# Second layer's modulation parts 2 to 5 by TensorE beside the convolution, fewer expert slots in the first sweep

## The chip, the core and the metric

The kernel runs on one NeuronCore of one Trainium2 chip. The metric is the device time of one execution in microseconds, as the median of several runs. All inputs are in the chip's memory (HBM) at the start, and the outputs are there at the end. The matrix products run on TensorE (PE), the element-wise work on VectorE (DVE), ScalarE (ACT) and GpSimd (POOL), and most transfers are issued by SyncE (SP).

## The reference

It is one step of a two-layer trunk on 384 tokens (128 context, 256 latent) of width 1024. What matters here:

```python
def adaln(cvec, w, b):
    m = jax.nn.silu(cvec) @ w + b                 # w: 1024 x 6144, two vectors cvec (c_ctx and c)
    return jnp.split(m[:, None, :], 6, axis=-1)
for l in range(DEPTH):                            # DEPTH = 2
    mp = adaln(c_ctx[None, :], mod_w[l], mod_b[l])
    ms = adaln(c, mod_w[l], mod_b[l])
    hp = modulate(rms_norm(xp, norm_mix_g[l]), mp[0], mp[1])
    ...                                           # layer 0: attention and pooling; layer 1: conformer_conv
    xp = xp + mp[2] * op
    hp = modulate(rms_norm(xp, norm_ffn_g[l]), mp[3], mp[4])
    xp = xp + mp[5] * peer(hp, ...)               # the same for the latent tokens with ms
def conformer_conv(h, w1, b1, w_dw, b_dw, ln_g, ln_b, w2, b2):
    a = h @ w1 + b1
    a = a[..., :CONV_DIM] * jax.nn.sigmoid(a[..., CONV_DIM:])
    a = depthwise_conv(a, w_dw, width=31) + b_dw
    a = jax.nn.silu(layer_norm(a, ln_g, ln_b))
    return a @ w2 + b2
```

`peer` picks 128 experts per token (8 heads, 16 each) out of 16384. It needs the dot product of the token with each expert's row of `peer_u`, and then the weighted sum of the rows of `peer_v`.

## The kernel before

The layout is transposed: `x[p, k, t]` holds channel 128 k + p of token t, so a row of 1024 channels is KC = 8 chunks of 128 partitions. Each engine has its own program, written out by hand. The order on an engine is the order of its code, and engines wait for one another by counting semaphores.

**Projections.** A block is a 128 x 1024 piece of a weight matrix (512 KB). SP loads it into one of four slots of `raw`, ACT rounds it into `w_hi`, POOL forms the rest `w_lo = raw - w_hi` (helper `low`), and PE multiplies: `project` issues 24 matmuls (8 chunks, 3 terms). The segments are in, out, wq0, u0, v0, w1 (16 blocks), w2 (8 blocks), wq1, u1, v1. In the u and v segments there are 128 blocks each.

**Experts of a layer.** For the 256 latent tokens the u and v tables are swept densely. In the u segment blocks 0 to 31 run while DVE finds the top keys (`top_keys`), blocks 32 to 95 run beside the building of the gate table (`with_table`), and blocks 96 to 127 are the tail (TAIL = 32). The v segment is the sweep: for each block DVE forms the weights `wf` from `a_in` and `g_in` (both read back from HBM), and PE runs `block_of`, 8 fp32 matmuls. For the 128 context tokens the experts' rows are fetched one slot at a time: POOL's `gather` is an indirect DMA of 128 rows of 8 KB (1 MB), into one of UVBUFS = 4 buffers, and it waits on `rows_used` until the row four slots earlier has been used. DVE's `step` makes the slot's dot product, ACT's `weight` bends and scales it, and DVE's `add_row` adds the row in the next step. Of the 128 slots of a layer 32 belong to the table blocks (one every two blocks), TAIL_STEPS to the tail and PER_EIGHT per eight blocks to the sweep.

**Modulation.** A block of `mod_w` is 512 KB: 128 output channels by 1024 inputs. DVE's `mod_group` takes the dot product of a block with one of the two conditioning vectors, held on all partitions in `c_all` (in `keys`), so a block takes two instructions; after four blocks `mod_bias` adds the bias. Part 0 of layer 0 (`shift_w`) is done by PE (`first_shift`). Of the other 88 blocks 32 are done in attention's stage (`mod_w`, slots in `hots`) and 56 in the first sweep (`mod_late`). DVE does 20 of the early blocks in `mod_four`, the last 12 in `late_mod`.

**Convolution (layer 1).** `blocks("w1")` projects 16 blocks in pairs. After each pair DVE's `product(k)` writes the gated chunk k into `a_pad`, and then issues 12 of its pending taps. The depthwise convolution of the 8 chunks is split: POOL does chunk 0 (31 taps of two instructions), DVE the chunks up to CONV_DVE, PE the rest, with 31 matmuls against diagonals that ACT makes. Then come the column sums for the layer norm (L1703 for the mean, L1707 for the squares), `blocks("w2")`, the next norm's column sums and `scores`.

```python
                for k in range(KC):
                    product(k)
                    if k >= CONV_POOL:
                        taps(12)
                taps(len(pending))
```

## Time and profile before

| what | value |
|---|---|
| median of 3 runs | 2520.72 us (2520.61 to 2526.32) |
| the profiled execution | 2531.83 us, span 2530.0 us |
| PE busy | 2294.8 us (91%) |
| DVE busy | 1735.4 us (69%) |
| POOL busy | 1180.4 us (47%) |
| ACT busy | 911.2 us (36%) |
| moved by DMA | 771.19 MB, 305 GB/s over the span |
| chain of waits | PE 55%, DMA 17%, DVE 13%, POOL 6% |

The shares are averages over stages with different limits, so each stage is read by itself, with the windows view (busy time of every engine in a stretch, the clock granted to TensorE, the share of time in which the 16 DMA engines were busy, and the rate). Matmul records overlap: the time from one start to the next is the pace, and the duration is the latency.

### The profile page before, as it was taken

What the parts mean: (1) busy time and instruction counts of PE and PEld (TensorE: products, weight loads), DVE (VectorE), ACT (ScalarE), POOL (GpSimd) and SP (SyncE); (2) the same over time, 40 slices, a digit from 0 to 9 for tenths busy, and PEclk for the clock granted to TensorE, in tenths of its full rate; (3) what the DMA queues carried; (4) which work ended last, traced back from release to release, by engine and by line L of the source; (5) the groups of instructions that cost most, each with busy time, mean ns of one, the idle gap of its engine ahead of it and who ended that gap; (6) DMA issues with size and microseconds to landing.
All of it is one profiled execution on the core that took longest, in us unless ns stands there. A gap on an engine that the chain in (4) does not pass through costs nothing.

```text
span 2530.0 us, 38376 instructions
## 1 busy us (share of the span) xinstructions
PE 2294.8 (91%) x11829; PEld 1693.0 (67%) x11829; DVE 1735.4 (69%) x3913; ACT 911.2 (36%) x1694; POOL 1180.4 (47%) x673
## 2 busy tenths in 40 slices
PE   6687999999998888888989889999999989999998
PEld 3676999999983333333459479989999944444443
DVE  7986798888435766677757856898885345545555
ACT  3253445666541111111033354656666410000002
POOL 2623487777782222222219635677777831111110
PEclk8898999999998999999999999999999999999999
DMA  7423368999999999999953023579999999999995
GB/s 300 158 77 125 109 225 286 381 390 375 379 412 398 400 396 402 386 394 401 394 187 122 9 67 117 183 254 369 383 386 376 391 366 400 400 398 408 400 399 188
DMA packets 195783, 771.19 MB, mean 305 GB/s; under 512 B 21728, under 2 KB 22880, under 8 KB 160224
## 3 DMA queue, kind: packets, MB, share of 16 engines
q1 hardware_dynamic: 120512, 402.81, 42.8%
q0 software_dynamic: 36864, 268.45, 26.8%
q10 hardware_dynamic: 38304, 98.71, 10.0%
q8 instruction: 45, 0.74, 0.1%
q14 instruction: 58, 0.48, 0.1%
HBM read 701.08 MB, written 68.81 MB: 304 GB/s over the span
## 4 chain that ended last, share of the span: by engine, by line
PE 55%; DMA 17%; DVE 13%; POOL 6%; issue 6%; ACT 2%; SPq 0%; ACTq 0%; DVEq 0%; POOLq 0%
PE ps L1785 26%; DMA raw<-in_v 12%; PE ps L1548 7%; PE ps L1549 7%; PE ps L1550 7%; POOL w_lo L602 5%; PE ps L1767 4%; DMA raw<-in_u 4%; DVE ps L1284 2%; DVE ps L1365 1%; DVE work L1367 1%; DVE ga L1084 1%; PE ps L1720 1%; ACT w_hi L728 1%; POOL work L674 1%
## 5 line engine op out<-in xcount | busy, mean ns | idle before, releaser
L602 POOL TENSOR_TENSOR w_lo<-raw,w_hi 128x1024 fp32r<-128x1024 f32 x330 | 802.9, 2440 | 514.1 <-ACT w_hi L728 511.6
L1785 PE MATMUL ps<-raw,work 128*128 128x512 f32 x2048 | 917.0, 608 | 92.5 <-DMA raw<-in_v 81.9
L1785 PEld LDWEIGHTS ps<-raw,work 128*128 128x128 f32 x2048 | 394.7, 195 | 613.5 <-issue 578.4
L1548 PE MATMUL ps<-h_hi,w_hi 128*128 128x256 f32 (+1 forms) x2560 | 773.9, 302 | 30.1 <-POOL w_lo L602 29.5
L1549 PE MATMUL ps<-h_lo,w_hi 128*128 128x256 f32 (+1 forms) x2560 | 754.0, 295 | 0.0
L1550 PE MATMUL ps<-h_hi,w_lo 128*128 128x256 f32 (+1 forms) x2560 | 753.8, 294 | 0.0
L1548 PEld LDWEIGHTS ps<-h_hi,w_hi 128*128 128x128 f32 x2560 | 491.9, 192 | 42.6 <-POOL w_lo L602 38.7
L1549 PEld LDWEIGHTS ps<-h_lo,w_hi 128*128 128x128 f32 x2560 | 492.5, 192 | 0.0
L1550 PEld LDWEIGHTS ps<-h_hi,w_lo 128*128 128x128 f32 x2560 | 491.4, 192 | 0.0
L728 ACT ACTIVATE w_hi<-raw 128x1024 fp32r<-128x1024 f32 x330 | 347.7, 1056 | 125.0 <-DMA raw<-in_u 49.0
L973 ACT ACTIVATE wgt<-dots (+1 forms) x256 | 53.2, 208 | 764.0 <-DVE uv_stat L1426 223.3
L620 POOL DMA_INDIRECT work<-in_uv,picked x64 | 73.7, 1151 | 245.4 <-DVE ps L1418 236.4
L620 POOL DMA_INDIRECT hots<-in_uv,picked x64 | 73.9, 1155 | 243.9 <-DVE ps L1418 232.8
L1445 DVE TENSOR_SCALAR hots<-ps,work 128x128 f32<-128x128 f32 x512 | 173.7, 401 | 0.0
L1469 DVE TENSOR_TENSOR work<-work,w_hi 128x256 f32<-128x256 f32 x128 | 53.7, 423 | 170.4 <-PE ps L1785 119.7
L993 ACT ACTIVATE work<-ps 128x512 f32<-128x512 f32 x128 | 145.8, 1139 | 66.9 <-PE ps L1767 65.0
L1469 DVE TENSOR_TENSOR work<-work 128x256 f32<-128x256 f32 x128 | 53.5, 423 | 166.9 <-PE ps L1785 125.5
L956 ACT ACTIVATE ga<-ps 128x256 f32<-128x256 f32 x256 | 97.7, 382 | 180.0 <-PE ps L1550 169.8
L1084 DVE CUSTOM_DVE_ANT_0 ga<-work,keys 128x1024 bf16<-128x1024 f32 x112 | 136.3, 1217 | 19.0 <-DMA work<-in_mod_w 11.7
L620 POOL DMA_INDIRECT hf<-in_uv,picked x64 | 71.9, 1124 | 152.6 <-DVE ps L1418 148.7
L1441 DVE TENSOR_TENSOR hots<-ps,work 128x512 f32<-128x512 f32 x128 | 87.9, 687 | 79.8 <-PE ps L1767 79.8
L620 POOL DMA_INDIRECT uv_stat<-in_uv,picked x64 | 71.5, 1117 | 141.5 <-DVE ps L1418 137.9
(199 smaller groups left out, 2524.7 us busy)
## 6 DMA issues: line engine op xcount, KB each, us to landing
raw<-in_u SPq DMA_DIRECT2D x256, 512.0 KB
raw<-in_v SPq DMA_DIRECT2D x256, 512.0 KB
a_dram<-ga ACTq DMA_DIRECT2D x128, 256.0 KB
g_dram<-work ACTq DMA_DIRECT2D x16, 2048.0 KB
work<-a_dram ACTq DMA_DIRECT2D x120, 256.0 KB
work<-in_mod_w SPq DMA_DIRECT2D x56, 512.0 KB, 14.5
hots<-in_mod_w SPq DMA_DIRECT2D x32, 512.0 KB, 3.6
raw<-in_wq SPq DMA_DIRECT2D x32, 512.0 KB
```

The costliest lines, as they stand in the source:

```text
L602: nc.gpsimd.tensor_tensor(w_lo[:, m % RING, :], raw[:, m % RING, :], w_hi[:, m % RING, :].bitcast(F32), ALU.subtract).then_inc(lo_ready, 1)
L620: nc.gpsimd.indirect_dma_start(out=uv_rows[q % UVBUFS], out_offset=None, in_=io[f"uv{layer}"], in_offset=bass.IndirectOffsetOnAxis(ap=pick ...
L728: nc.scalar.activation(w_hi[:, m % RING, :], raw[:, m % RING, :], ACT.Copy).then_inc(hi_ready, 1)
L993: nc.scalar.activation(stage[:, s, :, tok:tok + TOK].rearrange("p k t -> p t k"), ps[:, ACC, :].rearrange("p (t k) -> p t k", k=N_KEYS), A ...
L1084: nc.vector.tensor_tensor_reduce(unread[:, g, :], ring[:, k, :], c_all[:, g, :], 1.0, 0.0, ALU.mult, ALU.add, accum_out=sums[:, k, g:g + 1 ...
L1445: last = ts(oh1[:, b, q, :], iota_p, col_key[:, 0, tok], col_g[:, tok], ALU.is_equal, ALU.mult)
L1469: tt(wf[:, j % WBUFS, :].rearrange("p (c t) -> p c t", t=CHUNK), a_in[:, j % (2 * A_PAIRS), :].rearrange("p (c t) -> p c t", t=CHUNK), g_i ...
L1548: mm(out, w_hi[:, s, cols], h_hi[:, k, first:], start=n == 0, stop=False)
L1549: mm(out, w_hi[:, s, cols], h_lo[:, k, first:], start=False, stop=False)
L1550: last = mm(out, w_lo[:, s, cols], h_hi[:, k, first:], start=False, stop=n == KC - 1)
L1767: last = mm(ps[:, ACC, q * P:(q + 1) * P], oh2[:, b, q, :], oh1[:, b, q, :], start=True, stop=True)
L1785: last = mm(ps[:, Y_DENSE[NT - ND_TILES + t] + half, :], wf[:, b, t * P:(t + 1) * P], raw[:, s, half * 512:(half + 1) * 512], start=first, ...
```

## The change

Six things change together.

1. Parts 2 to 5 of layer 1's modulation (32 blocks) are no longer summed by DVE in the first sweep. A new array `part_w` holds them with inputs on the partitions, and PE's new `part_chunks` multiplies each chunk (128 inputs x 1024 outputs, 8 matmuls of 128 x 128 fp32 weights against two columns, `cvec`). Four chunks stand before w1, eight singly behind w1's blocks 5 to 12, eight before the mean, four before w2 and eight before layer 1's wq. SP loads them into five slots in `work`.
2. DVE's new `part_taken` adds the bias from PSUM. PE waits for the last one (`parts_taken`) before the wq1 projection.
3. Layer 0's sweep keeps 24 blocks of modulation instead of 56, two groups per four v blocks.
4. CONV_DVE is 7 instead of 6: DVE convolves six chunks, PE one, POOL one.
5. In layer 0 the sweep has 4 expert slots per eight blocks instead of 5, and the tail 32 instead of 16. Layer 1 stays.
6. `mod_four` reads the first vector from PSUM (`c_ps`), where ACT writes a second copy of it.

```diff
-CONV_DVE = 6
+CONV_DVE = 7
...
-SLOT_AT = (0, 2, 4, 5, 7)
-PER_EIGHT = len(SLOT_AT)
...
+SLOT_AT = ((0, 2, 4, 6), (0, 2, 4, 5, 7))
+PER_EIGHT = tuple(len(a) for a in SLOT_AT)
+TAIL_STEPS = tuple(SLOTS - TABLE_STEPS - N_KEYS // 8 * per for per in PER_EIGHT)
...
+SUM_PARTS = (1, 2, 3, 4, 5, 6, 7)
+PE_PARTS = (8, 9, 10, 11)
+PSLOTS = 5
+CHUNKS_NORM, CHUNKS_W1, CHUNKS_MEAN, CHUNKS_W2, CHUNKS_WQ = (range(a, b) for a, b in ((0, 4), (4, 12), (12, 20), (20, 24), (24, 32)))
+SUM_BLOCKS = len(SUM_PARTS) * KC
...
+            def part_chunks(chunks):
+
+                for n in chunks:
+                    since(sp, part_done, n - PSLOTS + 1)
+                    sp.dma_start(part_w[:, n % PSLOTS, :], one(io["part_w"], n)).then_inc(part_loaded[n % PSLOTS], 16)
...
+                    sp.wait_ge(rows_used, SLOTS)
+                    part_chunks(range(0, 5))
+                    stream("w1", RING, 1, 1)
+                    for n in range(5, 16):
+                        part_chunks([n])
+                        stream("w1", n, 1, 1)
...
+            nc.scalar.activation(c_ps, c_all[:, 0, :], ACT.Silu).then_inc(c_ready, 1)
...
-                        mod_group(i, MSLOTS, 0, k, g)
+                        mod_group(i, MSLOTS, 0, k, g, first=c_ps)
...
+            def part_taken(part, bank, col):
+
+                dve.wait_ge(part_done, (part - PE_PARTS[0] + 1) * KC)
+                cols = slice(part * KC, (part + 1) * KC)
+                return tt(mod[:, cols, :], ps[:, bank, col:col + 2 * KC].rearrange("p (a b) -> p a b", b=2),
+                          broad(mod_b[:, cols], [P, KC, 2], 2), ALU.add)
...
+                if layer:
+                    part_taken(6 + 5, ACC + 3, 0).then_inc(parts_taken, 1)
...
+            def part_chunks(chunks):
+
+                for n in chunks:
+                    pe.wait_ge(part_loaded[n % PSLOTS], 16 * (n // PSLOTS + 1))
+                    bank, col = ((ACC + 1, 0), (ACC, CONV_OUT + 1), (ACC + 2, 0), (ACC + 3, 0))[n // KC]
+                    k = n % KC
+                    for o in range(KC):
+                        last = mm(ps[:, bank, col + 2 * o:col + 2 * o + 2], part_w[:, n % PSLOTS, o * P:(o + 1) * P],
+                                  cvec[:, k, :], start=k == 0 and o == 0, stop=k == KC - 1 and o == KC - 1)
+                    last.then_inc(part_done, 1)
...
                 column_sums(2 * layer + 1)
+                if layer:
+                    part_chunks(CHUNKS_WQ)
+                    pe.wait_ge(parts_taken, 2)
                 scores(layer)
```

What stands on PE in w1 behind block 5 (L1885 is the new `part_chunks`, L1595 to L1597 are `project`; before, the block's last matmul was followed by the next block's first):

```order
L1595 MATMUL ps<-h_hi,w_hi 128x384
L1596 MATMUL ps<-h_lo,w_hi 128x384
L1597 MATMUL ps<-h_hi,w_lo 128x384
L1885 MATMUL ps<-cvec,work 128x2 [waits part_loaded4]
L1885 MATMUL ps<-cvec,work 128x2 x7
L1595 MATMUL ps<-h_hi,w_hi 128x384 [waits proj_taken,lo_ready]
L1596 MATMUL ps<-h_lo,w_hi 128x384
```

Eight narrow matmuls were put between two blocks. On PE ahead of layer 1's wq projection (L1643 are the column sums, L1612 is the first matmul of wq) there stands now, with five of the eight chunks not shown:

```order
L1643 MATMUL ps<-hf,ones 128x384 [waits sq_ready] x7
L1885 MATMUL ps<-cvec,work 128x2 [waits part_loaded4]
L1885 MATMUL ps<-cvec,work 128x2 x7
...
L1885 MATMUL ps<-cvec,work 128x2 [waits part_loaded0]
L1885 MATMUL ps<-cvec,work 128x2 x7
L1885 MATMUL ps<-cvec,work 128x2 [waits part_loaded1]
L1885 MATMUL ps<-cvec,work 128x2 x7
L1612 MATMUL ps<-h_hi,w_hi 128x384 [waits proj_taken,lo_ready,operand_ready,keys_loaded,parts_taken]
```

Before, the column sums were followed by wq's first matmul at once:

```order
L1588 MATMUL ps<-hf,ones 128x384 [waits sq_ready] x8
L1565 MATMUL ps<-h_hi,w_hi 128x384 [waits proj_taken,operand_ready,lo_ready,keys_loaded]
```

The first matmul of wq has the new wait `parts_taken`. What releases it stands on DVE behind all of the norm's instructions:

```order
L1198 SCALAR_TENSOR_TENSOR h_lo<-hf,mod,h_hi 128x128 [waits hi_part]
L1198 SCALAR_TENSOR_TENSOR h_lo<-hf,mod,h_hi 128x256
L1294 TENSOR_TENSOR mod<-ps,mod_b 128x16 [waits part_done,iota_ready]
L1425 MAX work<-work 128x8 [waits s_taken,parts_taken]
```

On POOL in layer 0's u segment, where the table blocks end and the tail begins, there stood before (L602 is `low`, L620 `gather`), and so on to the tail's end:

```order
L602 TENSOR_TENSOR w_lo<-raw,w_hi 128x1024 [waits hi_ready] x2
L620 DMA uv_stat<-in_uv0,picked 128x2048 [waits rows_used]
L602 TENSOR_TENSOR w_lo<-raw,w_hi 128x1024 [waits hi_ready] x2
L620 DMA hots<-in_uv0,picked 128x2048 [waits rows_used]
L602 TENSOR_TENSOR w_lo<-raw,w_hi 128x1024 [waits hi_ready] x2
```

And now (L629 and L647):

```order
L629 TENSOR_TENSOR w_lo<-raw,w_hi 128x1024 [waits hi_ready] x2
L647 DMA work<-in_uv0,picked 128x2048 [waits rows_used]
L629 TENSOR_TENSOR w_lo<-raw,w_hi 128x1024 [waits hi_ready] x2
L647 DMA uv_stat<-in_uv0,picked 128x2048 [waits rows_used]
L629 TENSOR_TENSOR w_lo<-raw,w_hi 128x1024 [waits hi_ready]
L647 DMA hots<-in_uv0,picked 128x2048 [waits rows_used]
L629 TENSOR_TENSOR w_lo<-raw,w_hi 128x1024 [waits hi_ready]
L647 DMA hf<-in_uv0,picked 128x2048 [waits rows_used]
L629 TENSOR_TENSOR w_lo<-raw,w_hi 128x1024 [waits hi_ready]
```

In the tail a gather now follows every block.

## Rows read from the trace of the kernel before

**Rows 1.** The page's chain that ended last, by engine and line.

```profile
PE ps L1785 26%; DMA raw<-in_v 12%; PE ps L1548 7%; PE ps L1549 7%; PE ps L1550 7%; POOL w_lo L602 5%; PE ps L1767 4%; DMA raw<-in_u 4%; DVE ps L1284 2%; DVE ps L1365 1%; DVE work L1367 1%; DVE ga L1084 1%; PE ps L1720 1%; ACT w_hi L728 1%; POOL work L674 1%
```

**Rows 2.** Windows view: stretch, length, busy us by engine (instructions), PE clock, DMA.

```profile
1323.00:1386.00 63.00, 61.66 (x344) 59.12 (x343) 45.57 (x89) 22.06 (x30) 60.47 (x40) 1.00 0.36 116
...
655.00:757.00 102.00, 93.16 (x731) 90.77 (x730) 36.83 (x46) 46.26 (x88) 85.62 (x46) 0.97 1.00 400
757.00:775.00 18.00, 10.76 (x26) 4.50 (x25) 4.58 (x7) 6.35 (x10) 1.21 (x1) 0.87 0.98 379
775.00:1240.00 465.00, 400.05 (x865) 170.99 (x865) 321.54 (x536) 50.52 (x149) 107.18 (x69) 0.93 1.00 397
1240.00:1298.60 58.60, 58.60 (x138) 26.02 (x139) 42.97 (x69) 7.34 (x23) 10.23 (x7) 1.00 0.85 326
...
2042.60:2451.60 409.00, 389.22 (x889) 167.76 (x889) 212.08 (x326) 35.78 (x144) 68.32 (x71) 0.99 1.00 396
2451.60:2510.20 58.60, 58.60 (x138) 26.03 (x139) 29.22 (x44) 5.56 (x20) 6.16 (x7) 1.00 0.73 277
```

**Rows 3.** The page's DMA issues: count, size, median us to landing.

```profile
work<-in_mod_w SPq DMA_DIRECT2D x56, 512.0 KB, 14.5
```

**Rows 4.** Timeline (start, length) of one gather in layer 0's tail, and its first reader.

```profile
724.16 0.95 POOL L620 DMA_INDIRECT work<-in_uv,picked  x1
...
734.11 1.22 DVE L1426 SCALAR_TENSOR_TENSOR work<-work,ps 128x1024 f32<-128x1024 f32 x1 [0.50 <-DMA work<-in_uv,picked]
```

**Rows 5.** Timelines of DVE and POOL after 55 us, and PE's longest wait there.

```profile
55.83 1.22 DVE L1084 CUSTOM_DVE_ANT_0 ga<-hots,keys 128x1024 bf16<-128x1024 f32 x1
56.97 3.37 DVE L1084 CUSTOM_DVE_ANT_0 ga<-hots,keys 128x1024 bf16<-128x1024 f32 x1
...
56.16 9.77 POOL L602 TENSOR_TENSOR w_lo<-raw,w_hi 128x1024 fp32r<-128x1024 f32 x3 [15.67 <-ACT w_hi L728]
...
PE ps L1598 <- DVE work L1192: 19.3, 1, 19.3
```

**Rows 6.** First_shift's eight narrow matmuls (L1817): windows view and weight loads' timeline.

```profile
40.50:42.50 2.00, 1.94 (x16) 1.86 (x16) 2.00 (x3) 0.00 (x0) 0.00 (x0) 1.00 1.13 369
...
40.86 1.53 PEld L1817 LDWEIGHTS ps<-ident,work 2*128 2x128 f32 x13
```

**Rows 7.** Timelines: two neighbouring chunks of a block on PE, two blocks on POOL.

```profile
1519.15 0.33 PE L1548 MATMUL ps<-h_hi,w_hi 128*128 128x384 f32 x1
...
1519.67 0.33 PE L1548 MATMUL ps<-h_hi,w_hi 128*128 128x384 f32 x1
...
1357.70 2.40 POOL L602 TENSOR_TENSOR w_lo<-raw,w_hi 128x1024 fp32r<-128x1024 f32 x1
...
1362.31 2.39 POOL L602 TENSOR_TENSOR w_lo<-raw,w_hi 128x1024 fp32r<-128x1024 f32 x1
```

**Rows 8.** Timelines of DVE and POOL at the end of the convolution.

```profile
1388.40 10.35 DVE L1284 SCALAR_TENSOR_TENSOR ps<-work,dw,ps 128x399 f32<-128x399 f32 x19
...
1435.08 0.57 DVE L1288 TENSOR_TENSOR work<-ps,work 128x399 f32<-128x399 f32 x1
...
1431.58 0.89 POOL L676 TENSOR_TENSOR work<-work 128x399 f32<-128x399 f32 x1
```

**Rows 9.** Timelines from layer 1's second column sums to the third block of wq.

```profile
1499.86 0.56 DVE L1128 TENSOR_SCALAR uv_stat<-ps 128x384 f32<-128x384 f32 x1 [2.83 <-PE ps L1588]
...
1514.15 0.74 DVE L1164 SCALAR_TENSOR_TENSOR h_lo<-hf,mod,h_hi 128x128 fp32r<-128x128 f32 x2
...
1507.14 0.66 PE L1565 MATMUL ps<-h_hi,w_hi 128*128 128x384 f32 x1 [7.32 <-DVE h_lo L1164]
...
1518.52 0.45 PE L1548 MATMUL ps<-h_hi,w_hi 128*128 128x384 f32 x1 [1.03 <-POOL w_lo L602]
```

**Rows 10.** Timeline of PE at the start of w1 and of w2.

```profile
1314.79 0.66 PE L1565 MATMUL ps<-h_hi,w_hi 128*128 128x384 f32 x1 [8.33 <-DVE h_lo L1164]
...
1456.66 0.66 PE L1565 MATMUL ps<-h_hi,w_hi 128*128 128x384 f32 x1 [7.78 <-DVE h_lo L1173]
```

More of the change, by code:

```diff
@@ L100 @@
 TABLE_STEPS = GBLOCKS // 2
-SLOT_AT = (0, 2, 4, 5, 7)
-PER_EIGHT = len(SLOT_AT)
-SWEEP_STEPS = N_KEYS // 8 * PER_EIGHT
-TAIL_STEPS = SLOTS - TABLE_STEPS - SWEEP_STEPS
-TAIL_EVERY = TAIL // TAIL_STEPS
+SLOT_AT = ((0, 2, 4, 6), (0, 2, 4, 5, 7))
+PER_EIGHT = tuple(len(a) for a in SLOT_AT)
+TAIL_STEPS = tuple(SLOTS - TABLE_STEPS - N_KEYS // 8 * per for per in PER_EIGHT)
+TAIL_EVERY = tuple(TAIL // steps for steps in TAIL_STEPS)
 STAIR = (4, 16)
 STAIRS = STAIR[0] * TOPK + (TOPK - STAIR[0]) * STAIR[0]
-assert TAIL_STEPS * TAIL_EVERY == TAIL and PER_EIGHT * (TURN // 8) % UVBUFS == 0
+assert all(steps * every == TAIL for steps, every in zip(TAIL_STEPS, TAIL_EVERY))
+assert all(per * (TURN // 8) % UVBUFS == 0 for per in PER_EIGHT)
 WBUFS = 4
@@ L352, in build @@
         shift_done = sem("shift_done")
+        part_loaded = [sem(f"part_loaded{k}") for k in range(PSLOTS)]
+        part_done = sem("part_done")
+        parts_taken = sem("parts_taken")
         mod_summed = sem("mod_summed")
@@ L704, in _ @@
                     low(R0[u] + b, M0[u] + b)
-                    if b % (2 if b < UBLOCKS + GBLOCKS else TAIL_EVERY) == 0:
+                    if b % (2 if b < UBLOCKS + GBLOCKS else TAIL_EVERY[layer]) == 0:
                         gather(layer, q)
@@ L785, in gated @@
                 m0 = M0[name]
-                act.wait_ge(mod_ready, [MOD_EARLY - 2 * KC, SUM_BLOCKS][layer] // MSLOTS)
+                if layer == 0:
+                    act.wait_ge(mod_ready, (MOD_EARLY - 2 * KC) // MSLOTS)
+                else:
+                    act.wait_ge(parts_taken, 1)
                 with act.Fori(0, 2) as i:
@@ L1006, in experts @@
                     plain(0, UBLOCKS + GBLOCKS + j, 1)
-                    if j % TAIL_EVERY == TAIL_EVERY - 1:
-                        weight(0, 0, TABLE_STEPS + j // TAIL_EVERY)
+                    if j % TAIL_EVERY[layer] == TAIL_EVERY[layer] - 1:
+                        weight(0, 0, TABLE_STEPS + j // TAIL_EVERY[layer])
                 v0 = M0[f"v{layer}"]
@@ L1073, in _, with mod_group @@
             dve.wait_ge(first_loaded, 5 * 16)
-            def mod_group(i, step, block, k, g, ring=mod_w):
+            def mod_group(i, step, block, k, g, ring=mod_w, first=None):
                 if k == 0 and g == 0:
@@ L1083, in mod_group @@
                 since(dve, mod_summed, i * (2 * step) + (2 * (block + k) + g - 1))
-                nc.vector.tensor_tensor_reduce(unread[:, g, :], ring[:, k, :], c_all[:, g, :], 1.0, 0.0,
+                nc.vector.tensor_tensor_reduce(unread[:, g, :], ring[:, k, :],
+                                               c_all[:, g, :] if g or first is None else first, 1.0, 0.0,
                                                ALU.mult, ALU.add, accum_out=sums[:, k, g:g + 1]).then_inc(mod_summed, 1)
@@ L1308, in convolution @@
                 pipelined(scaled, low_operand)
+                settle(part_taken(6 + 3, ACC, CONV_OUT + 1))
+                settle(part_taken(6 + 4, ACC + 2, 0))
+                mod_scales([3])
                 for k in range(KC):
@@ L1451, in one_hots @@
                 rounds(dve, GBLOCKS // (2 * SETS), table_rows, peel=True)
-                with dve.Fori(0, TAIL_STEPS // 4) as i:
+                with dve.Fori(0, TAIL_STEPS[layer] // 4) as i:
                     for j in range(4):
@@ L1479, in turn @@
                                     dve.wait_ge(a_stored[s], 16 * (N_KEYS // 4))
-                            block = MOD_EARLY - MSLOTS + j // 8 * MSLOTS
-                            mod_group(i, TURN // 8 * MSLOTS, block, j % 8 // 2, j % 2, mod_late)
-                            if j % 8 == 7:
-                                mod_bias(i, TURN // 8 * MSLOTS, block)
+                            block = MOD_EARLY + (span - 1) * MSLOTS
+                            mod_group(i, 2 * MSLOTS, block, j % SPAN // 4, j % 4 // 2, mod_late)
+                            if j % SPAN == SPAN - 1:
+                                mod_bias(i, 2 * MSLOTS, block)
                         if final and layer == 0 and j == SPAN + 8:
@@ L1569, in project_pair, with blocks @@
                             last.then_inc(block_done, 1)
-            def blocks(name, chunks=()):
+            def blocks(name, chunks=(), beside=()):
                 m, r = M0[name], R0[name]
@@ L1580, in blocks @@
                     project(0, 4, m + j, r + j)
+                if beside:
+                    for j in range(4, dict(SEGMENTS)[name]):
+                        project(0, 4, m + j, r + j)
+                        if j - 5 in range(len(beside)):
+                            part_chunks(beside[j - 5:j - 4])
+                    return
                 with pe.Fori(1, dict(SEGMENTS)[name] // 4) as i:
@@ L1681, in convolution @@
             def convolution():
-                blocks("w1")
+                part_chunks(CHUNKS_NORM)
+                blocks("w1", beside=CHUNKS_W1)
                 for c in range(KC - CONV_DVE):
```

78 lines of the change are left out of this document (47 added, 31 removed).

## Prediction

> **What bounds the kernel now.** I read the chain of waits first. Its two largest entries are PE's dense sweep of the v tables (L1785, 26%) and the loads of those blocks (12%); the w1/w2/wq and u projections, POOL's `w_lo` and DVE's convolution taps (L1284) follow [rows 1]. So the kernel has no single bound, and I read each stage touched in the windows view. In layer 0's tail of the u segment (655 to 757 us) the DMA engines are busy all the time at 400 GB/s, while PE is busy 93 of 102 us. The sweep that follows has the DMA share at 0.98 to 1.00 and 379 to 397 GB/s up to 1240 us; PE is busy 400 of 465 us. Only the last 58.6 us are PE alone. Layer 1's sweep, which has no modulation blocks in it, has the same shape, but its DMA-bound stretch is 409 us instead of 18 + 465 = 483 us [rows 2]. In w1 (1323 to 1386 us) DMA is at 0.36; PE is busy 61.7 and POOL 60.5 of 63 us, so both are full and anything put on PE there shows [rows 2]. The change takes bytes out of the stage that DMA bounds and puts work on PE and DVE in a stage that they bound.
>
> **The sweep of layer 0.** It loses 32 modulation blocks of 512 KB (of the 56 that are loaded there [rows 3]), 16.8 MB, and 16 of its expert slots of 1 MB, another 16.8 MB. From 757 to 1240 us it moved 18 x 379 + 465 x 397, which is 191.4 MB. The last stretches of the two layers differ by 326 - 277 = 49 GB/s over 58.6 us, 2.9 MB [rows 2], so that much of the modulation lay behind 1240 us, where it cost nothing. What is left is 191.4 - 33.6 + 2.9 = 160.7 MB, at 397 GB/s 405 us, 78 us less. PE's floor is below it: the last stretch does 138 records, 17.25 blocks, in 58.6 us, 3.40 us a block, so the other 110.75 blocks need 377 us. Layer 1 moved 409 x 396, 162 MB, in 409 us with the same PE work [rows 2]. I take its 409 us: 483 - 409, **-74 us**. Bounds: -60, if the gap between PE's floor and the data being this small brings waits of 14 us more, and -99 at PE's floor with its 7 us stall at the start. DVE's removed groups were not what PE waited for (DVE busy 322 of 465 us [rows 2]), so they count for nothing apart.
>
> **The tail of layer 0.** The 16 slots go here, one per block instead of one per two. The stage is at DMA's limit: 16.8 MB at 400 GB/s are +42 us on 102 [rows 2]. There is a second limit. A gather waits until the row four slots earlier has been added, and that addition stands behind the next slot's dot product, which needs that slot's rows. So four periods hold one period, the latency of a gather, the dot product and the addition (1.2 us each) and the issue (0.95 us). The gather issued at 724.16 us ended DVE's wait at 734.1 us, a latency of 9.9 us [rows 4]. The period is then (9.9 + 3.4)/3 = 4.4 us, the tail 142 us against 102: +40 us. Data and loop give the same, and where two limits coincide a little is lost: **+44 us**. Bounds: +15 us, POOL's issues alone (16 x 0.95), and +63 us at a latency of 12 us.
>
> **The convolution stage.** A chunk is eight matmuls of 128 columns of fp32 weights against two columns. The nearest row is first_shift's: eight such matmuls, only with 2 partitions instead of 128. They show as 16 records, busy 1.94 us at a granted clock of 1.00 (2.4 GHz), and 13 of their weight loads took 1.53 us, 0.118 us each [rows 6]. I take 16 x 0.118, 1.9 us a chunk. Below it could go to 16 x 0.05 = 0.8 us, should loads with 128 partitions overlap better than these, above to 3.8 us at the 1.2 GHz level. The Trainium skill, page "TensorE: Matmul & The Clock Gate", section "LDWEIGHTS (loading the stationary operand)", says that a load takes its columns divided by 1.2 in ns and that the number of partitions doesn't matter; by that 16 loads are 1.7 us. Its section "Back-to-back issue gap" gives about 25 ns for a matmul with up to 64 moving columns, by which a chunk would be 0.4 us and this stage 12 us cheaper; the row, at 0.118 us, speaks for the loads.
>
> - In w1 PE's pace is 0.52 us for three matmuls, 4.16 us a block; POOL's is 1362.31 - 1357.70 = 4.61 us [rows 7]. POOL's pace ruled the last eight blocks, which leaves PE 8 x 0.45 = 3.6 us. Eight chunks are 15.2 us, so w1 ends 15.2 - 3.6, **+12 us** later. Bounds +3 and +27.
> - DVE's sixth chunk: 31 taps of 10.35/19 = 0.545 us and an addition of 0.57 us [rows 8], **+17.5 us**. It isn't hidden: each product is followed by 12 taps, so 72 are done before the last product either way, and behind it stand 114 instead of 83. DVE finished at 1435.65 us and is what the mean waits for. POOL's last tap ended at 1432.5 us, three us earlier [rows 8]; it is not pushed by the change as far as DVE, so it stays hidden. PE's chunk saved was hidden too, and PE's eight chunks ahead of the mean (15 us) fit into that wait.
> - wq of layer 1: before, PE began with the first operand (1507.14 us) and reached the third block at 1518.52 us. The column sums were there at 1499.86 us [rows 9]. Eight chunks end at 1499.9 + 15.2 = 1515.1 us. The last `h_lo` ends at 1514.9 us, then comes `part_taken`, some 0.5 us with its semaphores. PE starts at 1515.6 us and has 48 matmuls of 0.173 us, 8.3 us, so the third block begins at 1523.9 us: **+5.5 us**. Behind that wait stand all of wq and DVE's `top_keys`. Bounds +5 and +20.
> - The four chunks ahead of w1 (7.6 us) go into PE's 8.33 us wait, the four ahead of w2 into one of 7.78 us [rows 10]. Without that cover each would cost up to 7.6 us. Their 2.6 MB are loaded just behind the sweep, with the DMA nearly free. Small DVE instructions (three `part_taken`, a `mod_scales`): **+0.5 us**.
>
> Sum of the stage: 12 + 17.5 + 5.5 + 0.5 = +35.5 us.
>
> **The vector in PSUM.** After 55 us a `mod_group` takes 1.22 us, but 3.37 us when it meets a POOL `low` (three of which took 9.77 us at that time); eight of the 24 groups before the rope do. PE waits 19.3 us for DVE here [rows 5], so DVE time counts. With one input in PSUM the first group of each pair should run beside POOL; the second then still waits for what is left of 2.4 us. Eight times (2.15 - 1.25) are 7 us, and the `mod_bias` instructions meet POOL less often: **-8 us**. Bounds 0 (PSUM doesn't help) and -19. The Trainium skill, page "SBUF — State Buffer", section "Who interferes with whom", says that a DVE instruction with two SBUF inputs contends with a GpSimd instruction that reads SBUF, and one with at most one SBUF input doesn't; by that the first bound falls away. ACT's extra copy stands ahead of the first norm, where it delays `c_all` by about 1 us; DVE's first groups there wait for the norm's statistics anyway, so I count it at nothing, at most 1 us.
>
> **Sum.** -74 + 44 + 35.5 - 8 = -2.5 us. The durations come from an execution of 2531.83 us (span 2530.0 us), 11 us above the median of 2520.72 us. In its own time the sum is 2529.3 us; against the median it is 2520.7 - 2.5 = **2518 us**. A measurement can tell this kernel from no change from about 0.3%, 7.6 us.
>
> **Rivals.**
> - Faster: the costs in the convolution and the tail overlap better than counted. With chunks of 0.8 us w1 costs 3 us and the stage 26.5 us; with a tail at +35 us the sum is -74 + 35 + 26.5 - 8 = -20.5 us, 2500 us. For it speaks that the tail's PE floor is far off; against it the record of 0.118 us and a DMA share of 1.00 [rows 2, 6].
> - Slower: the gather loop becomes the tail's bound. Its place is POOL's wait for `rows_used`, behind which every `w_lo` of the u segment stands. Each us of latency costs 32/3 = 10.7 us. At 12 us the tail takes 32 x 5.13 = 164 us, +62, and the total is +15.5 us, 2536 us; it decides from a latency of about 11 us. For it: more gathers in flight make each slower. Against it: the loop slows its own traffic.
> - Slower: a chunk costs 3.8 us, because PE falls to 1.2 GHz or loads of 128 partitions take longer. w1 is +27 us, wq +20 us, the two covers are overrun by 7 us each, though the projections behind them wait for operands anyway (+5 together): +70 against +35.5, 2552 us. Against it: the row, and the clock of 1.00 in w1 [rows 2, 6].
> - The sweep keeps its waits: modulation loads stand in SP's queue among the v blocks, and only 60 us are won. +14 us, 2532 us. Against it: the queue held more than twice as many before, at the same 397 GB/s [rows 2].
>
> **How the numbers follow.** The forecast, gains and costs balancing within 0.3% (2511 to 2526 us), has 0.40; the first rival 0.33; the gather loop 0.12; dear chunks 0.07; a sweep that keeps its waits 0.06; anything else 0.02, half of it on each side. So faster by over 0.3% is 0.34, within 0.3% 0.40, slower 0.26. The range that leaves out 0.2 goes from the first rival to the second: 2499 to 2539 us.
>
> **What the profile after would show.** The sweep: v blocks from start to end some 467 us instead of 541, and a DMA share still near 1.00. The tail: 142 to 148 us, loads of u still at 400 GB/s; if POOL waits long for DVE's addition at a lower rate, it is the loop. w1: PE full, the narrow matmuls at 0.11 to 0.12 us per record, and the last product some 12 us later. From there to the end of DVE's taps 65 instead of 48 us. wq: PE's first matmul about 8 us behind the first operand. Before the rope: fewer 3.37 us groups, and PE's 19.3 us wait down by 7 or 8 us. I am wrong if a chunk is far from 1.9 us, if the tail's period is far from 4.5 us, or if PE starves in the sweep.

## The result and the profile after

The changed kernel takes 2530.51 us by the median (10 runs, 2524.61 to 2536.95), the kernel before on the same chip 2522.1 us (10 runs). The ratio is 1.0032, 95% interval 1.0017 to 1.0046: about 8 us slower, right at the bound of what can be told from no change. I had forecast 2518 us and an even balance.

The profiled execution took 2534.0 us, its span is 2532.2 us; before it was 2530.0. So the two traces differ by only 2.2 us. The profile before was of an execution some 10 us above its median, the one after only 3.5 us above; where those 6 us lie can't be read from one trace of each. The experiments give more traces of the same stages; the paragraph on the sum comes back to it. For the stages I take marks that both traces have: DVE's first MAX8 of each layer's `top_keys`, PE's first and last matmul of the v table, PE's column sums.

| stage, us | before | after | difference | forecast |
|---|---|---|---|---|
| start to layer 0's `top_keys` | 249.0 | 239.2 | -9.8 | -8 |
| to the first v matmul (u table, tail) | 508.7 | 542.6 | +33.9 | +44 |
| layer 0's sweep | 540.9 | 473.4 | -67.4 | -74 |
| convolution stage, to layer 1's `top_keys` | 232.1 | 276.4 | +44.3 | +35.5 |
| all behind it | 999.3 | 1000.5 | +1.2 | 0 |

The windows view of the sweep after, in two stretches cut as in [rows 2] (columns as there):

```profile
781.80:1196.60 414.80, 390.67 (x888) 167.75 (x889) 236.21 (x386) 50.27 (x131) 59.27 (x58) 0.99 1.00 390
1196.60:1255.20 58.60, 58.60 (x138) 25.88 (x137) 27.68 (x40) 4.57 (x16) 3.74 (x4) 1.00 0.74 263
```

They hold 414.8 x 390 + 58.6 x 263, 177 MB. PE is busy 449 of 473 us, and DMA still shows a share of 1.00: both limits are now close to the time.

The convolution stage, by the windows around `part_chunks` (L1885) and the first two blocks of wq: ahead of w1, in w1, ahead of the mean, ahead of w2, ahead of wq, wq.

```profile
1263.10:1271.90 8.80, 8.80 (x66) 8.80 (x65) 4.94 (x12) 5.50 (x10) 4.09 (x2) 0.79 0.99 380
1299.60:1344.00 44.40, 44.40 (x303) 44.39 (x302) 29.65 (x57) 9.75 (x12) 38.90 (x27) 1.00 0.54 189
1378.50:1403.70 25.20, 25.20 (x129) 25.20 (x129) 25.04 (x47) 0.00 (x0) 18.53 (x16) 0.55 0.57 189
1432.00:1442.00 10.00, 10.00 (x65) 10.00 (x63) 5.49 (x11) 8.03 (x14) 0.00 (x0) 0.67 0.00 0
1483.40:1507.50 24.10, 24.10 (x129) 24.08 (x127) 13.03 (x36) 9.57 (x20) 2.34 (x1) 0.57 0.41 132
1507.90:1519.50 11.60, 11.39 (x48) 11.08 (x49) 0.00 (x0) 0.61 (x2) 0.00 (x0) 0.74 0.00 0
```

Read the clock, third from the end, with the first number. PE is busy all the time in each of the first five, yet the granted clock is 1.00 (2.4 GHz) only in w1, where dense blocks stand between the chunks. Where chunks stand alone it is at the 1.2 GHz level for part or most of the time (a mean of 0.55 to 0.79), and eight of them take 25.2 and 24.1 us, 3.0 to 3.15 us each.

PE's timeline from the end of its taps (L1745) to w2 shows what the mean waits for, and DVE's the end of layer 1's second norm:

```profile
1378.49 25.33 PE L1885 MATMUL ps<-cvec,work 128*128 128x2 f32 x128 [0.68 <-ACT work L935]
1403.68 6.49 PE L1759 MATMUL ps<-work,ones 128*128 128x399 f32 x12
1421.51 3.03 PE L1759 MATMUL ps<-work,ones 128*128 128x399 f32 x4 [11.34 <-DVE work L1329]
...
1498.76 0.74 DVE L1198 SCALAR_TENSOR_TENSOR h_lo<-hf,mod,h_hi 128x128 fp32r<-128x128 f32 x2 [0.21 <-ACT h_hi L806]
1507.68 0.17 DVE L1294 TENSOR_TENSOR mod<-ps,mod_b 128x16 f32<-128x16 f32 x1 [8.17 <-PE ps L1885]
```

The last `h_lo` (L1198) is there at 1499.5 us, but `part_taken` waits 8.17 us more for PE's chunks, and PE's wq waits for it. At the beginning of the kernel none of the 20 groups (L1117) with one input in PSUM is held up (1.21 to 1.22 us each), and PE's wait for DVE is 14.5 us where it was 19.3 [rows 5]:

```profile
54.35 2.67 DVE L1117 CUSTOM_DVE_ANT_0 ga<-hots,keys 128x1024 bf16<-128x1024 f32 x1
56.94 1.21 DVE L1117 CUSTOM_DVE_ANT_0 ga<-hots,ps 128x1024 bf16<-128x1024 f32 x1
58.09 2.28 DVE L1117 CUSTOM_DVE_ANT_0 ga<-hots,keys 128x1024 bf16<-128x1024 f32 x1
```

```profile
PE ps L1653 <- DVE work L1226: 14.5, 1, 14.5
```

### The profile page after: what moved, and what is told of

Its sections match the earlier page's. It is cut to its first block, busy times and chain, and to the rows that moved or that the text cites. A ratio compares the mean times of both kernels' runs of the same rounds, so it can differ in the third digit from the quotient of the medians.

```text
span 2532.2 us, 38923 instructions
## 1 busy us (share of the span) xinstructions
PE 2345.5 (93%) x12279; PEld 1766.5 (70%) x12279; DVE 1676.8 (66%) x3813; ACT 900.8 (36%) x1663; POOL 1135.1 (45%) x673
## 4 chain that ended last, share of the span: by engine, by line
PE 61%; DMA 16%; DVE 14%; issue 4%; POOL 2%; ACT 1%; SPq 0%; ACTq 0%; DVEq 0%; POOLq 0%
PE ps L1842 27%; DMA raw<-in_v 9%; PE ps L1595 8%; PE ps L1596 8%; PE ps L1597 8%; PE ps L1824 4%; DMA raw<-in_u 3%; DVE ps L1325 2%; POOL w_lo L629 2%; PE ps L1885 2%; DMA hots<-in_uv,picked 1%; DVE ps L1414 1%; DVE work L1416 1%; PE ps L1777 1%; PE ps L1643 1%
## 5 line engine op out<-in xcount | busy, mean ns | idle before, releaser
L629 POOL TENSOR_TENSOR w_lo<-raw,w_hi 128x1024 fp32r<-128x1024 f32 x330 | 796.5, 2420 | 558.4 <-ACT w_hi L755 557.2
L1842 PE MATMUL ps<-raw,work 128*128 128x512 f32 x2048 | 898.5, 599 | 45.3 <-DMA raw<-in_v 34.6
L1595 PE MATMUL ps<-h_hi,w_hi 128*128 128x256 f32 (+1 forms) x2560 | 777.5, 304 | 51.2 <-POOL w_lo L629 50.1
L1842 PEld LDWEIGHTS ps<-raw,work 128*128 128x128 f32 x2048 | 387.8, 191 | 554.7 <-issue 520.8
L1597 PE MATMUL ps<-h_hi,w_lo 128*128 128x256 f32 (+1 forms) x2560 | 756.8, 296 | 0.0
L1595 PEld LDWEIGHTS ps<-h_hi,w_hi 128*128 128x128 f32 x2560 | 494.9, 193 | 62.9 <-POOL w_lo L629 60.4
L1597 PEld LDWEIGHTS ps<-h_hi,w_lo 128*128 128x128 f32 x2560 | 494.6, 193 | 0.0
L647 POOL DMA_INDIRECT hots<-in_uv,picked x64 | 65.7, 1026 | 237.8 <-DVE ps L1467 227.2
L647 POOL DMA_INDIRECT work<-in_uv,picked x64 | 61.5, 962 | 216.8 <-DVE ps L1467 205.0
L647 POOL DMA_INDIRECT uv_stat<-in_uv,picked x64 | 60.5, 945 | 173.6 <-DVE ps L1467 170.2
L1824 PE MATMUL ps<-hots 128*128 128x128 f32 x1024 | 135.2, 275 | 0.0
L647 POOL DMA_INDIRECT hf<-in_uv,picked x64 | 61.1, 954 | 158.4 <-DVE ps L1467 154.7
```

Of the source, the lines that this page charges most:

```text
L629: nc.gpsimd.tensor_tensor(w_lo[:, m % RING, :], raw[:, m % RING, :], w_hi[:, m % RING, :].bitcast(F32), ALU.subtract).then_inc(lo_ready, 1)
L647: nc.gpsimd.indirect_dma_start(out=uv_rows[q % UVBUFS], out_offset=None, in_=io[f"uv{layer}"], in_offset=bass.IndirectOffsetOnAxis(ap=pick ...
L1595: mm(out, w_hi[:, s, cols], h_hi[:, k, first:], start=n == 0, stop=False)
L1597: last = mm(out, w_lo[:, s, cols], h_hi[:, k, first:], start=False, stop=n == KC - 1)
L1824: last = mm(ps[:, ACC, q * P:(q + 1) * P], oh2[:, b, q, :], oh1[:, b, q, :], start=True, stop=True)
L1842: last = mm(ps[:, Y_DENSE[NT - ND_TILES + t] + half, :], wf[:, b, t * P:(t + 1) * P], raw[:, s, half * 512:(half + 1) * 512], start=first, ...
```

## The experiments

Ratios are to the kernel before, run on the same chip in each case. "Stage" is the convolution stage of the table, last v matmul to layer 1's `top_keys`.

**e1: the chunks ahead of wq go into w2.**

```diff
+                if behind:
+                    for j in range(4, 8):
+                        project(0, 4, m + j, r + j)
+                        part_chunks(behind[2 * (j - 4):2 * (j - 3)])
+                    return
...
-                blocks("w2")
+                blocks("w2", behind=CHUNKS_WQ)
...
-                    part_chunks(CHUNKS_WQ)
                     pe.wait_ge(parts_taken, 2)
```

> The changed kernel, with the eight part_chunks that stood in front of wq placed behind w2's last four blocks, two behind each (their loads are all issued before wq's; the vector is taken at the same place as before). Clock theory: the eight cost 3.0 us each in front of wq (24.1 us for 128 records) because nothing but narrow matmuls runs there and the granted clock is 0.57; between dense blocks they should cost 1.85 us each as in w1, 14.8 us in w2, and PE then begins wq with its first operand and at a higher clock. w2 14.8 us longer, from the column sums to wq's third block 27 us shorter: about 10 to 13 us faster than the changed kernel, 2518 to 2521 us by the median of the changed kernel, so no different from the kernel before. Rival, that a chunk of 128-partition loads costs 3 us wherever it stands: w2 24 us longer, at most 3 us gained. Rival, that DVE's residuals or POOL's w_lo already set w2's pace and hide the chunks: over 16 us faster.

Measured: 2543.91 us, ratio 1.0093 [1.0068, 1.0118], slower than the changed kernel by 0.6%. PE's timeline of it:

```profile
1475.49 3.63 PE L1888 MATMUL ps<-cvec,work 128*128 128x2 f32 x32
1483.24 3.63 PE L1888 MATMUL ps<-cvec,work 128*128 128x2 f32 x32
...
1527.07 0.69 PE L1610 MATMUL ps<-h_hi,w_hi 128*128 128x384 f32 x1 [16.16 <-DVE mod L1292]
```

Windows view of its column sums (columns as above; the clock is 0.76):

```profile
1503.80:1511.00 7.20, 7.11 (x18) 3.70 (x17) 0.06 (x1) 0.00 (x0) 0.00 (x0) 0.76 0.00 0
```

The chunk price came out as the clock theory says, 1.82 us each beside dense blocks, and the second rival falls. My sum for wq was wrong: PE does not begin with its first operand, since `parts_taken` stands behind the whole of DVE's norm. It waits 16.16 us. From the column sums (1503.8 us) to the first block it is 23.3 us against 29.7 in the changed kernel and 12.6 before. But e1's column sums themselves took 7.1 us, against 5.3 in both other kernels at a clock of 1.00, so 1.8 us of its 23.3 are not the wait. The wait for DVE's whole norm costs 8.9 us of the changed kernel's 17.1 here, and the chunks' low clock the other 8.2. w2 pays 16.8 us for the eight chunks.

**e2: the first vector from SBUF again.**

```diff
-                        mod_group(i, MSLOTS, 0, k, g, first=c_ps)
+                        mod_group(i, MSLOTS, 0, k, g)
```

> The changed kernel, but mod_four reads the first conditioning vector from SBUF again, not from PSUM (ACT's copy stays). Theory: every group before the rope that meets GpSimd is held up again; top_keys of layer 0 starts 8 to 10 us later and the whole is 8 to 10 us slower than the changed kernel. Rival, that the 9.8 us came from the order of the loads or from ACT: 0 to 3 us slower, with the 3.4 us groups only half as many as before.

Measured: 2537.33 us, 1.0066 [1.0040, 1.0092]; `top_keys` starts at 249.0 us instead of 239.2. The interval just overlaps the changed kernel's; it is the trace that makes the difference clear.

**e3: layer 0's slots back.**

```diff
-SLOT_AT = ((0, 2, 4, 6), (0, 2, 4, 5, 7))
+SLOT_AT = ((0, 2, 4, 5, 7), (0, 2, 4, 5, 7))
```

> The changed kernel with layer 0's expert slots placed as in the kernel before (five per eight v blocks, one per two blocks of the tail). Bytes theory: tail and sweep are both at the DMA engines' limit, so 16.8 MB cost 41 us wherever they stand; the tail falls from 142 to 104 us, the sweep grows from 473 to 513 us: within 5 us of the changed kernel. Rival, that the sweep is by now so near PE's own pace that its DMA time has slack: the sweep grows by 25 us only, 13 us faster. Rival, that the gather loop costs the tail more than the bytes do: also faster, by the part of 38 us that the sweep doesn't take back.

Measured: 2514.89 us, 0.9978 [0.9962, 0.9994], 0.54% faster than the changed kernel. To the first v matmul it is 507.1 us (-35.5), the sweep 493.7 us (+20.3). The first rival holds: the bytes cost nearly their full price (41 us) in the tail and half of it in the sweep.

**e4: 17 taps behind each product in w1.**

```diff
-                        taps(12)
+                        taps(17)
```

> The changed kernel with 17 taps instead of 12 behind each product in w1, so that DVE uses the time that PE's part_chunks give it there (DVE is busy 29.6 of 45 us in w1's first part). The taps behind the last product fall from 102 to 67, by 35 x 0.545 = 19 us. Theory: DVE's last addition, which the mean waits for, comes 15 to 19 us earlier, but PE's eight part_chunks (25.3 us at a low clock) and twelve records of the mean end at 1410 us, so only the 11.3 us in which PE waits are won: 10 to 12 us faster than the changed kernel. Rival, that 17 taps delay the next product and so PE in w1: each product comes 1 us later, w1 6 us longer, a gain under 6 us.

Measured: 2515.2 us, 0.9979 [0.9965, 0.9993]. DVE's last addition is now ahead of PE's last sum, and PE no longer waits for it; PE's timeline:

```profile
1388.10 24.04 PE L1885 MATMUL ps<-cvec,work 128*128 128x2 f32 x128 [0.68 <-ACT work L935]
1411.99 7.49 PE L1759 MATMUL ps<-work,ones 128*128 128x399 f32 x16
```

The stage takes 268.5 us, 7.9 less; the medians say 13. Three traces have this stage as in the changed kernel (276.4, 279.2 and 280.9 us in after, e3 and e2) and two as here (268.5 and 267.4 in e4 and e8), which makes 11. As expected, PE's chunks became the bound. A little of the rival is there too: the last product comes 3.2 us behind PE's last block of w1, where it was 0.8.

**e5: a dense matmul behind each chunk ahead of wq.**

```diff
                     last.then_inc(part_done, 1)
+                    if chunks == CHUNKS_WQ:
+                        mm(ps[:, ACC + 1, 0:T], ones[:, :], x[:, 0, :], start=True, stop=True)
```

> The changed kernel, with one useless matmul of 384 columns (ones by x, fp32, into a bank that nobody reads) behind each of the eight part_chunks in front of wq. Clock theory: a chunk takes 3.0 us there and 1.84 in w1 because narrow matmuls alone don't hold the granted clock; eight dense ones cost 8 x 0.66 = 5.3 us themselves, but if they hold the clock the stretch is 8 x 2.5 = 20 us instead of 24.3, and wq starts at 2.4 GHz: 4 to 8 us faster than the changed kernel, although it does more work. Rival, that the chunks wait for something else (their loads, the weights' path): 24 + 5 to 10 us, the kernel 5 to 10 us slower.

Measured: 2540.34 us, 1.0067 [1.0049, 1.0086]. The added matmuls did not hold the clock. Windows view, of the chunks' whole stretch and of two of them, and PE's timeline:

```profile
1489.30:1522.90 33.60, 33.60 (x144) 29.59 (x143) 13.22 (x37) 9.57 (x20) 2.34 (x1) 0.55 0.27 94
1505.00:1514.40 9.40, 9.40 (x38) 8.19 (x37) 0.47 (x2) 0.64 (x1) 2.34 (x1) 0.50 0.15 56
```

```profile
1500.27 3.41 PE L1885 MATMUL ps<-cvec,work 128*128 128x2 f32 x16
1503.55 1.63 PE L1889 MATMUL ps<-x,ones 128*128 128x384 f32 x2
```

The first chunk took 1.84 us at a clock of 1.00, the second 2.59 at 0.67, and the other six 3.41 us each at 0.50; the added matmul's two records last 1.63 us there (0.66 in the column sums at 1.00). The result is the rival's by its size, but its reason (loads, the weights' path) isn't shown by it: the clock is low here too. That one such matmul behind each chunk is too little is what this run shows, no more.

**e6: the kernel before with the vector in PSUM alone**; **e7: that and the slots by layer**, all modulation still on DVE.

```diff
+            nc.scalar.activation(c_ps, c_all[:, 0, :], ACT.Silu).then_inc(c_ready, 1)
...
+                        mod_group(i, MSLOTS, 0, k, g, first=c_ps)
```

> The kernel before, with the first vector in PSUM and nothing else (the later wait on the vectors counts the extra signal). If this part is worth by itself what undoing it cost the changed kernel (ratio 1.0066 against 1.0032, 8.6 us; top_keys 10 us earlier): 9 to 10 us faster than the kernel before, 2510 us. Rival, that a DMA-bound stage later takes the gain back: within 3 us of before.

> The kernel before with the vector in PSUM and the slots by layer (16 slots moved from layer 0's sweep to its tail), all modulation still on DVE in the sweep. Theory: in the changed kernel the slots' move costs 17 us net (tail +37, sweep -20), because there the sweep is already near PE's own pace once the modulation blocks are gone; with these still in it the sweep is bound by data alone and gives back the full 41 us: within 5 us of the kernel with the vector alone. Rival, that the move costs 17 us whatever else the sweep holds (gathers in the tail delay the u loads): 13 to 17 us slower than that kernel.

Measured: e6 2512.3 us, 0.9962 [0.9948, 0.9976]; e7 2505.28 us, 0.9932 [0.9915, 0.9950]. The sweeps in the windows view, first e6's, then e7's two stretches:

```profile
748.20:1227.20 479.00, 409.01 (x888) 174.77 (x888) 326.29 (x542) 56.49 (x158) 108.55 (x70) 0.93 1.01 399
1227.20:1285.80 58.60, 58.57 (x137) 26.01 (x138) 43.06 (x69) 7.34 (x23) 10.22 (x7) 1.00 0.85 325
```

```profile
783.70:1221.50 437.80, 400.22 (x888) 172.56 (x888) 294.47 (x502) 48.94 (x128) 88.33 (x57) 0.96 1.02 404
1221.50:1280.10 58.60, 58.58 (x138) 26.02 (x139) 38.71 (x63) 6.34 (x19) 7.62 (x5) 1.00 0.78 294
```

With the modulation still in it, the sweep gives back 41 us for the 16 slots (537.7 to 496.5) and the stretch ahead of it grows by 35. The theory holds, and the move is even a small gain there, 7 us by the medians, though the intervals just overlap. Against e7 the changed kernel is what the modulation's move and DVE's sixth chunk cost: 1.0032 against 0.9932, 25 us slower. By the two traces that is -23 us in the sweep and +45.5 us in the stage (230.9 to 276.4).

**e8: e3 and e4 together.**

> The changed kernel with both edits that helped it alone: layer 0's slots back at five per eight blocks, and 17 taps behind each product in w1. They lie in different stages (tail and sweep; convolution), so the gains of 13.6 and 13.4 us should add: 27 us faster than the changed kernel, ratio to before about 0.992, 2501 us. Rival, that an earlier sweep end meets later loads and gives part back: 2508 us.

Measured: 2501.94 us, 0.9919 [0.9901, 0.9937]. The gains add. Its interval overlaps e7's.

**e9: only two of the four parts by TensorE, all 16 chunks in waits**, five convolution chunks on DVE and two on PE as before; **e10: the same with layer 0's slots back.**

```diff
-SUM_PARTS = (1, 2, 3, 4, 5, 6, 7)
-PE_PARTS = (8, 9, 10, 11)
+SUM_PARTS = (1, 2, 3, 4, 5, 6, 7, 8, 9)
+PE_PARTS = (10, 11)
...
-CONV_DVE = 7
+CONV_DVE = 6
```

> Only parts 4 and 5 of the second layer's modulation by TensorE (16 chunks: four ahead of w1, eight ahead of the mean, four ahead of w2, all in waits of PE), parts 2 and 3 on VectorE in the sweep; the vector in PSUM and the slots by layer as in the changed kernel, five convolution chunks on VectorE as before, nothing in w1 or in front of wq. Theory: the costs of the changed kernel's convolution stage are those chunks that stand outside waits, and VectorE's sixth chunk; here the stage takes what it took before, within 5 us (232 us from the last v matmul to layer 1's top_keys; PE's two tap chunks end some 31 us before DVE's last addition, and eight chunks at 3.0 us with seven sums fit in just). The sweep loses 8.4 MB against the kernel with vector and slots alone and takes 478 to 484 us instead of 496. Sum: 12 to 18 us faster than that kernel's 2505 us, about 2490 us. Rival, that even hidden chunks delay the stage by their clock: the mean and w1 start at 1.2 GHz and the stage is 10 us longer: 2500 us.

> The same with layer 0's slots as in the kernel before. If the slots' move and the removal of modulation draw on the same slack, with 8.4 MB less in the sweep it is half used up: tail 37 us shorter, sweep 25 to 35 us longer: 2 to 12 us faster than with the move. Rival, that they are independent: equal to it within 3 us, or slower by 6 as between the kernel with vector and slots and that with the vector alone.

Measured: e9 2514.54 us, 0.9980 [0.9963, 0.9997]; e10 2515.15 us, 0.9979 [0.9962, 0.9996]. The sweep behaved (483.0 and 515.4 us), the stage did not: 256.9 us in both, 25 more than before. PE's timeline of e9:

```profile
1360.59 41.73 PE L1735 MATMUL ps<-work,hots 128*128 128x399 f32 x124
1403.01 23.20 PE L1875 MATMUL ps<-cvec,work 128*128 128x2 f32 x128 [0.68 <-ACT work L928]
```

I had taken half the price for PE's taps: two chunks of them are 41.7 us, not 21. In the kernel before they end at 1429.2 us, 6.5 us ahead of DVE's last addition [rows 8]; its timeline there:

```profile
1387.47 41.73 PE L1689 MATMUL ps<-work,hots 128*128 128x399 f32 x124
1429.05 4.47 PE L1703 MATMUL ps<-work,ones 128*128 128x399 f32 x12
```

There was never room for eight chunks in front of the mean unless PE gave up a chunk of taps. e9 and e10 are alike in time, as e10's rival says. The traces show its theory all the same: with the slots back the stretch ahead of the sweep is 36.8 us shorter and the sweep 32.4 us longer, between the 41 of e7 and the 20 of e3. The net 4 us are too few for the medians.

**e11: the changed kernel with the convolution's chunks as before, five on DVE, two on PE, one on POOL.**

```diff
-CONV_DVE = 7
+CONV_DVE = 6
```

> The changed kernel with five convolution chunks on VectorE and two on TensorE, as before; everything else kept. DVE's last addition comes 17.6 us earlier, but PE now has 10.8 us more of taps ahead of its eight part_chunks at 3.1 us each: chunks end at 1414.6 us instead of 1403.7, the sums behind them at 1422. So PE takes the place of DVE as what the mean waits for, and only 4 to 5 us are won, within what can be told from no change. Rival, that the sixth chunk is a pure loss: 15 to 17 us faster. Rival, that the two chunks' banks or the diagonal weights hold PE up: slower.

Measured: 2536.18 us, 1.0069 [1.0040, 1.0098]; not faster, and by the medians 9 us slower, with intervals that just overlap. The reason is the same. PE has 20 us more of taps, its chunks end at 1420.4 instead of 1403.8 us, and counted from the last v matmul the mean's sums end 5.8 us later. So DVE's sixth chunk buys more on PE than it costs on DVE, as long as the eight chunks stand ahead of the mean.

**e12: e8 with the chunks laid out by their prices.**

```diff
-((0, 4), (4, 12), (12, 20), (20, 24), (24, 32))
+((0, 4), (4, 22), (22, 22), (22, 26), (26, 32))
...
-                        taps(12)
+                        taps(12 if k < 3 else 24)
```

> The kernel with the slots back and 17 taps (2501.9 us), with the 32 chunks laid out by what they cost at each place: four ahead of w1 and four ahead of w2 as before, eighteen in w1 (two behind each of nine blocks) instead of eight, none ahead of the mean instead of eight, six ahead of wq instead of eight; 12 taps behind w1's first products and 24 behind the later ones. Theory, from this case's chunk prices (1.84 us beside dense blocks, 3.0 to 3.2 us where narrow matmuls stand alone, and in front of wq hidden up to DVE's own 18 us there): w1 18 us longer, the wait for the mean 25 us shorter, wq 6 us shorter, 11 to 14 us faster: 2489 us, ratio 0.987. Rival, that PE was not what the mean waited for once DVE has 17 taps a product, or DVE now is (42 taps, 23 us, behind the last product, against PE's 21 us of taps): 2 to 6 us faster. Rival, that twice the chunk loads in w1 hold up the loads of its blocks: no gain or slower.

Measured: 2514.82 us, 0.9967 [0.9950, 0.9983], 12 us slower than e8 where I expected as much faster. The window of its nine chunk pairs in w1, and PE's timeline at the mean:

```profile
1287.20:1365.40 78.20, 78.20 (x482) 78.19 (x480) 53.84 (x102) 11.63 (x13) 43.51 (x30) 0.83 0.53 173
```

```profile
1376.54 21.05 PE L1743 MATMUL ps<-work,hots 128*128 128x399 f32 x62 [1.04 <-DVE work L1302]
1398.27 4.29 PE L1757 MATMUL ps<-work,ones 128*128 128x399 f32 x12 [0.68 <-ACT work L933]
1414.52 1.70 PE L1757 MATMUL ps<-work,ones 128*128 128x399 f32 x2 [11.96 <-DVE work L1327]
```

Two chunks behind each block were too many for the clock: 0.83 in w1. From its first to its last block w1 took 115.7 us, 31.5 more than in e8, where I had counted 18. PE is busy 78.20 of 78.20 us here, so it was not the loads that held it up. And I had counted 42 taps behind the last product; the 24 that follow it at once come on top, 66 in all, so that DVE is 12 us late. In front of wq the layout did what it should: from the column sums to the first block 22.2 us instead of 29.

## Why the prediction was wrong, point by point

**Where it failed: the convolution stage's wq term.** "Eight chunks end at 1499.9 + 15.2 = 1515.1 us" and "48 matmuls of 0.173 us" gave +5.5 us. Measured is +17.3: from the start of the column sums to wq's third block 41.3 us (1478.2 to 1519.5) against 24.0. The chunks took 24.25 us instead of 15.2 (+9), at a low granted clock. The two blocks behind them took 11.6 us instead of 8.3 (+3.3). That second part is not a cost of the chunks: the same two blocks took 11.4 us in the kernel before (clock 0.83) and 11.6 in e7 (0.73), where no chunk stands ahead of them. I had priced them at the full clock's pace, as a gain of 3 us on before. I had read the price of a chunk from a row at full clock [rows 6] and given the 1.2 GHz case 0.07. That price was right in one place (w1) and wrong in four. About half of the term would be there at full clock too, since PE waits for DVE's whole norm (e1). The prediction named its own sign of being wrong, a chunk far from 1.9 us, and that is what the trace shows. The sum of the stage was +35.5, measured +44.3; this term alone is more than the difference.

The Trainium skill, page "TensorE: Matmul & The Clock Gate", section "What's actually happening", says that the array's clock is throttled by default and that activity releases it, by how busy the engine has been. The rows agree only if busy there does not mean what the profile's busy column does: with 24.10 us busy of 24.10 the granted clock was 0.57.

**w1: right.** The last product ended 101.4 us behind the last v matmul, before 89.9: +11.5, forecast +12. A chunk took 1.84 us, forecast 1.9. No run came near the lower bound of 0.8 us, whose 0.05 us per record comes from no row.

**DVE's sixth chunk: right in size, wrong in what I said of its cover.** The last addition came another 17.6 us later. But "PE's chunk saved was hidden too" missed what it was for: those 20.9 us of PE hold the eight chunks, which take 25.3 us and not 15. Where PE keeps them as taps, the eight chunks push the mean's sums out: 5.8 us later than after in e11, 26.9 us later than before in e9.

**The covers ahead of w1 and w2: not quite held.** w1 began 16.5 us behind the sweep, before 16.2; but this trace is a lucky one. In ten others with four chunks there it was 16.4 to 19.1 us, in e6 and e7 without any 16.2. Ahead of w2 the four chunks took 10.4 us and the wait was 7.8: w2 began 10.1 us behind the sums of squares, before 7.8. That doesn't show in the sum because those sums took 5.6 us in this trace and 8.5 in the one before. The chunks are not the reason, since e6 without any has 5.6 us too.

**The tail: +34, forecast +44.** Both the data and the gather loop gave 40, and I added 4. The length that I worked out for the tail, 142 us, came out: from PE's first matmul of the u segment's block 96 to the first v matmul it is 141.6 us, and with a DMA share of 1.02 and a rate that didn't fall it is the data that set it, not the gather loop. What was wrong is what I took it from. By the same mark the tail before was 107.4 us and not 102, since the stretch that I read [rows 2] begins some 5 us into it; so +34, and e6 to e7 gives +34 too. The data say the same: 42.6 MB at 396 GB/s before, 58.3 MB at 412 after. The rate rose a little, and no loss is left over that two coinciding limits would have added.

**The sweep: -67, forecast -74**, within its bounds of -60 to -99. The reason that I gave for the bound was the right one, a gap between PE's floor and the data that becomes small. The runs show it as a curve. MB moved by the two stretches of the windows view and time of the sweep are 210 and 538 us (e6), 202 and 515 (e10), 194 and 496 (e7) or 494 (e3), 185 and 483 (e9), 177 and 473 (after). The first 16 MB bring 41 to 44 us, the next 17 MB 20 to 23 us; PE's own pace is 435 us. What the prediction did not see is what follows for the parts. The slots and the modulation are 16.8 MB each, and whichever goes second brings half. Neither is bad by itself for the sweep; together the slots' move costs 35 us in the tail for 20 in the sweep (e3).

**The vector in PSUM: -9.8, forecast -8.** e2 and e6 show it from both sides, 8.6 and 9.6 us by ratio. The Trainium skill's rule (page "SBUF — State Buffer", section "Who interferes with whom"), that one SBUF input doesn't contend, is borne out: 1.21 us beside POOL, where the other group of the pair, with both inputs in SBUF, took 2.28 to 2.67 us in the lines above. One of the signs was missed: PE's wait fell by 4.8 us and not by 7 or 8.

**The sum.** Each term was off by 2 to 10 us, and the errors in part cancelled: forecast -2.5, by the traces +2.2, by the medians +8.4. The 6 us between the last two are the spread of single traces. Where several traces have a stage's code in common, their means can be compared:

| stage, us | as before (traces) | as after (traces) | difference |
|---|---|---|---|
| start to layer 0's `top_keys` | 249.0 (2) | 239.7 (12) | -9.3 |
| to the first v matmul | 507.3 (6) | 542.7 (8) | +35.4 |
| layer 0's sweep | 539.3 (2) | 475.5 (6) | -63.8 |
| convolution stage | 230.7 (3) | 278.8 (3) | +48.1 |

They add up to +10.4 us, near the medians' +8.4. One stage alone spreads over up to 5 us, and all that stands behind it, the same code in all 14 traces, over 991.0 to 1000.5 us. So the trace after flattered the change in the sweep (-64 rather than -67, near the forecast's bound of -60) and in the convolution (+48 rather than +44). These two terms were too hopeful by 10 and 13 us. That the forecast missed the median by only 11 us is in part luck, since the tail came out 9 us cheaper than forecast.

## What to carry to other kernels

Moving bytes out of a DMA-bound stage pays in full only down to the next engine's pace; two edits that draw on the same slack must be priced together, and the runs of each with and without the other show it. Narrow matmuls don't only cost their own time: placed alone they let the clock fall, and what stands right behind them can pay too (12 records of the mean's sums took 6.49 us behind the chunks, 4.47 before), so put them one by one between dense blocks, and let the engine next to them use the longer stage (17 taps instead of 12 were worth 11 to 13 us). Before work is put "into a wait", look up when the engine before that wait really ends: here it was 6.5 us of room, and I had counted 31 for e9.

The best kernel of the study is e8, 0.8% faster than before; e7, without any of the modulation's move, is 0.7% faster. Their intervals overlap, so no run shows that moving the modulation to TensorE gains anything.
